# One decoder step on one core: the recurrence and the output projection in another order

## Chip, cores and metric

The kernel runs on one core of one Trainium2 chip. The metric is the device time of one execution in microseconds (us). PE is the matrix engine (PEld its weight loads), DVE the vector engine, ACT the engine for activations, POOL the fourth compute engine, and SP the queue from which all loads and stores are issued. Each engine runs its own program in the order in which it is written, and semaphores hold it until what it needs is there.

## What is computed

One layer of a decoder for 1024 prompt tokens and 8 sample tokens that share all weights. Width 1024, 4 heads of 128, a convolution of 31 taps over 512 channels, 32 experts in 4 groups.

```python
mod = silu(c) @ w_ada + b_ada                     # six rows: shift, scale, gate, twice
h = rms_norm(x, norm1_g) * (1 + sc1) + sh1
z = h @ w_in                                      # q k v o | i f | glu_a glu_b
# heads: per chunk of 128 tokens, state C (128 x 128), n, m for each head
w = exp(dmat - m_t); a_inter = exp(inter - m_t)
s = (q @ k.T) * w
num = s @ v + a_inter * (q @ C); den = sum(s) + a_inter * (q @ n)
hm = num / max(|den|, exp(-m_t))
C = decay * C + (wl * k).T @ v                    # n the same way
hm = layer_norm(hm, mh_norm_g) * sigmoid(o)
# convolution
u = glu_a * sigmoid(glu_b)
hc = silu(layer_norm(causal_conv_31(u) + b_dw))   # norm over the 512 channels
x = x + g1 * (concat(hm, hc) @ w_out)
h2 = rms_norm(x, norm2_g) * (1 + sc2) + sh2
x = x + g2 * hier_moe(h2)                         # best group, best two experts in it
y = rms_norm(x, final_g)
```

The new states, the last 30 convolution inputs and `y` are outputs, for both groups. The prompt starts from zero states; the sample group starts from given ones and takes one token per sequence.

## The kernel before

Tokens stand in 9 tiles: 8 of 128 prompt tokens and one of the 8 samples. The program goes through these stages.

- Conditioning, first norm, and turning `x` (to 54 us). After it `h` lies in SBUF as `hhi` and `hlo`, a coarse and a fine half of each number.
- Projection (54 to 377 us). `project(j)` on PE makes 128 columns of `z` for all 1032 tokens, in 144 matmuls of 344 columns (line 1870): three products of halves. Blocks 0 to 3 are glu_a, 4 to 7 glu_b, then 4 blocks each of q, k, v and o. For each block ACT makes `whi` from the loaded `wraw` (line 1612), DVE makes `wlo` (line 1756), and ACT copies the result out (line 1618). Both halves of the weights have two buffers, so `whi` of block j + 2 follows the end of block j. `z_done`, `whi_ready`, `wlo_ready`, `z_evac` count these steps. Two further groups of conditioning matmuls stand between blocks, and the gate projection behind block 11.
- Beside it on DVE: the 31 taps of the convolution for 4 channel blocks, 4 first taps (line 1781) and 120 of the form "times weight, plus sum" (line 1788), eight per projection block from block 10 on; and `gate_rows` (lines 347 to 374), the running sums and maxima of the gates, behind `wlo` of block 15. Its rows, after three exponentials on ACT, are turned on PE (line 1909) ahead of block 16.
- Reduction of the convolution (377 to 426 us): channel sums on PE with a matrix of ones (lines 719, 739), centring on DVE, squares and a norm on ACT, then a silu. The sigmoids are passes of their own over 4 blocks each.
- Recurrence and output projection (426 to 717 us), a loop over the chunks c. PE makes scores and decay (`inputs`), the part from the state (line 882), numerator (896) and state product (901), then the whole output projection of tile c - 1 (line 822, 32 records), turns the heads of chunk c (911) and `h2` of tile c - 2 (831), and runs the router of tile c - 3 (845). ACT scales the state's part (473, `n2s`), takes the tile's statistics (443 to 445) and copies `h2T` (451). DVE combines the heads, makes `x2 = x + g1 * y` (623, 625) and `h2` (637, 639).
- The sample group's steps hang in that loop as stages: queries against its state `C0` (line 779, 32 single columns), its norms in the small tile `sm`, the outer products (791) in chunks 3 to 6 and, in chunk 7, three broadcasts of modulation rows (762) into the place of `C0`, after the store of the new `C0`. The prompt's three broadcasts stand in chunk 0.
- Routing (730 to 771 us), experts (to 1128 us) and final norm, opened by the mark `stage1_over` on DVE (line 1158) that waits for all stores of this stage.

SP issues the loads in a fixed order too. Behind the projection: the convolution cache `crow`, `wout`, the router's weights and biases, `ntok`, the four parts of `C0`, and then for each tile the load of `x` and the stores of `x2` and `h2`.

Of the kernel before, what the change touches and what calls it, by code (L numbers as in the profile page):

```python
# [67 lines left out]
        "c9T_ps vT_ps gates_ps rowsT_ps mean_ps cT_ps tails_ps cmean_ps sumsq_ps n0T_ps vtok_ps "  # L68
        "qc_ps nnew_ps smean_ps svar_ps rank_ps"),
    "DVE": (  # L70
        "modr_zero dve_consts c9T_ready A1_ready u_ready rows_in csum_ready sB_ready centred conv_sum "
        "centred_s conv_scaled snew_ready sh_ready ssq_ready feats_ready mlstm_done stage1_over "
        "gmax_ready ediff_ready mask_ready glists_ready nov_ready experts_done"),
    "ACT": (
        "csilu softplus_ready srow_ready crstd_ready vtok_ready conv_done nnew_ready srstd_ready "
# [29 lines left out]
def build(nc, x_prompt, x_sample, c_prompt, c_sample, C0, n0, m0, cache, w_ada, b_ada, norm1_g, w_in,  # L105
# [10 lines left out]
    with ExitStack() as ctx:  # L116
# [74 lines left out]
        m0t = sb(st1, "m0t", [H, S])  # L191

# [33 lines left out]
        whi = sb(stB, "whi", [P, 2, KD, P], F32R)  # L226
        stB.close()
# [8 lines left out]
        utail = sb(st1, "utail", [PAD, CB * P])  # L236
        usam = sb(st1, "usam", [S, CB * P])
# [11 lines left out]
        featT = sb(st1, "featT", [P, 2, H, P])  # L249
        featS = sb(st1, "featS", [P, H, S])  # L250
        stL = ExitStack()
        crow = sb(stL, "crow", [4 * PAD, 2, CB * P])
        crstd = sb(stL, "crstd", [P, NTOK])
        cT = sb(stL, "cT", [P, CB, S, CW])
        cprod = sb(stL, "cprod", [P, CB, S, CW])
        stL.close()
        x2 = sb(st1, "x2", [P, 2, D])
        h2 = sb(st1, "h2", [P, D])
        h2T = sb(st1, "h2T", [P, KD, P])
        st1.close()  # L260
# [68 lines left out]
        TAILS, MEAN, YB, BB = 6, 6, 6, (6, 0)  # L329
# [5 lines left out]
        def bcs(i):  # L335

            return z[0:S, U0 + i, 0:D]
# [38 lines left out]
        def act_rest(act, chain):  # L376
# [4 lines left out]
            def conv_squares():  # L381

                act.wait_ge(step("tails_ps"), after("tails_ps"))
                act.activation(utail[:, :], ps[0:PAD, TAILS, :], ACT.Copy).then_inc(sem("tails_ready"), 1)
                act.activation(usam[:, :], ps[0:S, TAILS + 1, :], ACT.Copy).then_inc(sem("tails_ready"), 1)

                act.activation(z[:, U0:U0 + CB, PAD:SC], z[:, GB0:GB0 + CB, PAD:SC], ACT.Square).then_inc(sem("squares"), 1)
                act.wait_ge(step("centred_s"), after("centred_s"))
                act.activation(z[:, U0:U0 + CB, SC:ZW], z[:, GB0:GB0 + CB, SC:ZW], ACT.Square).then_inc(sem("squares"), 1)
                for b in range(H):  # L390
                    act.activation(z[:, O0 + b, PAD:ZW], z[:, O0 + b, PAD:ZW], ACT.Sigmoid).then_inc(sem("sig_o"), 1)
# [63 lines left out]
            for c in range(NC_):  # L455
# [11 lines left out]
                if c == 0:  # L467
                    conv_squares()
# [1484 lines left out]
```

## Time and profile before

| | us |
|---|---|
| runs shown | 1181.47, 1182.86, 1184.37 (median 1182.86) |
| the profiled execution | 1184.33 |
| its span, first to last instruction | 1182.2 |
| PE busy, share of the span | 961.1, 81% |
| DVE busy | 760.3, 64% |
| ACT busy | 502.6, 43% |
| mean granted clock of PE | 0.899 |

The profile gives, for an engine, each instruction's start and duration, and in brackets how long the engine was idle before it and what released it. A record of PE holds a matmul or a part of one. "Granted clock" is the share of full speed that PE was allowed in a stretch: 1.00 is 2.4 GHz, 0.50 is 1.2 GHz.

### The profile page before, as it was taken

The page shows a single profiled execution, that of the slowest core. Times are in us where ns is not written, and L with a number is a line of the kernel's source. Part 1 is how long each engine was busy: PE and PEld are TensorE (multiplying, and loading weights), DVE is VectorE, ACT ScalarE, POOL GpSimd, SP SyncE. Part 2 cuts the span into 40 slices and gives each one's busy share as a digit, 9 for nine tenths or more (in the row PEclk, how much of TensorE's full clock was granted, in tenths as well). Part 3 has the DMA queues.
Part 4 walks back from the last instruction along what each step waited for, and adds up shares of the span by engine and source line. Part 5 has one row for each costly group of instructions (what it writes and reads, how often), then busy time and mean ns, then how long its engine had stood idle before and what let it go on. Part 6 is the DMA issues. An engine that isn't in the chain of part 4 may idle for free. (4 is left out here: it accounts for less than half of the span.)

```text
span 1182.2 us, 12857 instructions
## 1 busy us (share of the span) xinstructions
PE 961.1 (81%) x5013; PEld 770.5 (65%) x5013; DVE 760.3 (64%) x937; ACT 502.6 (43%) x629; POOL 153.1 (13%) x120
## 2 busy tenths in 40 slices
PE   4599999996998779889993890579999999999800
PEld 2398989796997466546562430468888888887700
DVE  3520139499898551625653224879999999998568
ACT  4532231311211540422221010358888888887444
POOL 0100000000000000000000000013443343444300
PEclk9699999997999888979997895689999999999955
DMA  7935311103112420111113007748999999999266
GB/s 284 397 144 206 151 37 36 36 1 72 36 35 64 148 80 1 72 36 55 54 61 117 37 35 157 299 160 352 376 384 384 378 384 380 400 394 358 92 264 255
DMA packets 64758, 213.12 MB, mean 180 GB/s; under 512 B 13840, under 2 KB 34976, under 8 KB 46766
## 3 DMA queue, kind: packets, MB, share of 16 engines
q1 hardware_dynamic: 54334, 195.42, 44.2%
q0 software_dynamic: 10368, 16.93, 3.9%
q8 instruction: 38, 0.62, 0.2%
q14 instruction: 18, 0.15, 0.0%
HBM read 199.14 MB, written 34.49 MB: 198 GB/s over the span
## 5 line engine op out<-in xcount | busy, mean ns | idle before, releaser
L1171 DVE TENSOR_TENSOR elo<-eraw,ehi 128x2048 fp32r<-128x2048 f32 x72 | 161.4, 2283 | 0.0
L1788 DVE SCALAR_TENSOR_TENSOR z<-z,wdT 128x1024 f32<-128x1024 f32 x120 | 144.7, 1279 | 0.1
L1063 ACT ACTIVATE ehi<-eraw 128x2048 fp32r<-128x2048 f32 x72 | 134.0, 1909 | 4.9 <-DMA eraw<-in_w_up 2.5
L1870 PE MATMUL ps<-hhi,whi 128*128 128x344 f32 x576 | 124.8, 326 | 6.4 <-ACT hhi L1640 3.6
L1870 PE MATMUL ps<-hhi,wlo 128*128 128x344 f32 x576 | 124.1, 324 | 0.0
L1870 PE MATMUL ps<-hlo,whi 128*128 128x344 f32 x576 | 122.9, 322 | 0.0
L1618 ACT ACTIVATE z<-ps 128x1032 f32<-128x1032 f32 x24 | 24.8, 1034 | 218.3 <-PE ps L1870 218.3
L1870 PEld LDWEIGHTS ps<-hhi,whi 128*128 128x128 f32 x576 | 98.3, 191 | 8.9 <-issue 8.9
L1756 DVE TENSOR_TENSOR wlo<-wraw,whi 128x1024 fp32r<-128x1024 f32 x22 | 26.9, 1225 | 114.1 <-ACT whi L1612 114.1
L1870 PEld LDWEIGHTS ps<-hhi,wlo 128*128 128x128 f32 x576 | 99.4, 192 | 0.0
L1870 PEld LDWEIGHTS ps<-hlo,whi 128*128 128x128 f32 x576 | 97.3, 190 | 0.0
L1176 DVE TENSOR_TENSOR dlo<-draw,dhi 128x2048 fp32r<-128x2048 f32 x36 | 82.5, 2291 | 0.0
L1380 PE MATMUL ps<-ehi,xhi 128*128 128x512 f32 x288 | 76.7, 409 | 2.1 <-issue 2.1
L1014 POOL DMA_INDIRECT expert_results<-ysb,lists x27 | 72.4, 2681 | 35.4 <-ACT ysb L1089 35.4
L1004 POOL IOTA ioti<- 128x128 int32 x1 | 0.2, 240 | 563.2 <-DVE marks L1158 563.2
L1380 PE MATMUL ps<-ehi,xlo 128*128 128x512 f32 x288 | 72.4, 394 | 0.0
L1380 PE MATMUL ps<-elo,xhi 128*128 128x512 f32 x288 | 71.1, 389 | 0.0
L1069 ACT ACTIVATE dhi<-draw 128x2048 fp32r<-128x2048 f32 x36 | 69.6, 1933 | 0.0
L822 PE MATMUL ps<-wout,featT 128*128 128x512 f32 x128 | 63.1, 650 | 2.8 <-DVE x L625 2.8
L1295 DVE TENSOR_TENSOR xlo<-ps,xhi 128x1024 fp32r<-128x1024 f32 x36 | 44.1, 1225 | 32.0 <-ACT xhi L1073 32.0
L822 PE MATMUL ps<-wout,z 128*128 128x512 f32 (+1 forms) x144 | 63.3, 592 | 0.0
L1380 PEld LDWEIGHTS ps<-ehi,xlo 128*128 128x128 f32 x288 | 54.9, 191 | 12.2
(369 smaller groups left out, 1579.2 us busy)
## 6 DMA issues: line engine op xcount, KB each, us to landing
eraw<-in_w_gate SPq DMA_DIRECT2D x36, 1024.0 KB, 13.5
eraw<-in_w_up SPq DMA_DIRECT2D x36, 1024.0 KB, 16.5
draw<-in_w_down SPq DMA_DIRECT2D x36, 1024.0 KB, 17.1
wada<-in_w_ada SPq DMA_DIRECT2D x24, 1024.0 KB, 10.0
wraw<-in_w_in SPq DMA_DIRECT2D x12, 1024.0 KB, 5.3
y<-expert_results SPq DMA_DIRECT2D x8, 1024.0 KB, 7.9
xt<-in_x_prompt SPq DMA_DIRECT2D x8, 512.0 KB, 5.8
wout<-in_w_out SPq DMA_DIRECT2D x1, 4096.0 KB, 16.0
```

The source lines that it names most:

```text
L822: mm = pe.matmul(ps[0:n, bank + a, :], lhs, wout[:, k, a * 512:(a + 1) * 512], start=(k == 0), stop=(k == KD - 1))
L1014: pool.indirect_dma_start(out=ye_dram, in_=ysb[:, b, :], in_offset=None, out_offset=bass.IndirectOffsetOnAxis(ap=at, axis=0), bounds_check ...
L1063: act.activation(ehi[:, s % 2, i, :, :], eraw[:, s, i, :, :], ACT.Copy).then_inc(sem("ehi_ready"), 1)
L1069: act.activation(dhi[:, s % 2, :, :], draw[:, s, :, :], ACT.Copy).then_inc(sem("dhi_ready"), 1)
L1171: dve.tensor_tensor(elo[:, s, i, :, :], eraw[:, s, i, :, :], ehi[:, s % 2, i, :, :].bitcast(F32), ALU.subtract)\
L1176: dve.tensor_tensor(dlo[:, s, :, :], draw[:, s, :, :], dhi[:, s % 2, :, :].bitcast(F32), ALU.subtract)\
L1295: dve.tensor_tensor(xlo[:, b, :, :], ps[:, 0:2, :].rearrange("p a (k n) -> p (a k) n", k=4), xhi[:, b, :, :].bitcast(F32), ALU.subtract).t ...
L1380: mm = pe.matmul(ps[:, 2, :].rearrange("p (i f) -> p i f", i=2), x[:, b, k, :], w[:, :, k, :], start=(i + k == 0), stop=(i == 2 and k == K ...
L1618: act.activation(z[:, j, PAD:ZW].rearrange("p (c n) -> p c n", c=3), ps[:, 3 * v:3 * v + 3, 0:TW], ACT.Copy).then_inc(sem("z_evac"), 1)
L1756: dve.tensor_tensor(wlo[:, u, :, v * P:(v + 1) * P], wraw[:, u, :, v * P:(v + 1) * P], whi[:, v, :, :].bitcast(F32), ALU.subtract).then_in ...
L1788: dve.scalar_tensor_tensor(out=z[:, GB0 + b, PAD:SC], in0=z[:, U0 + b, w:w + T], scalar=wdT[:, b, w:w + 1], in1=z[:, GB0 + b, PAD:SC], op0 ...
L1870: mm = pe.matmul(ps[0:n, bank + c, 0:TW], w(k), h[:, k, c * TW:(c + 1) * TW], start=first, stop=last)
```

## The change

**Convolution.** ACT writes sigmoids straight out of the accumulators for blocks 4 to 7 and 20 to 23. DVE forms the gate product of each channel block when that block is out, and taps begin with the first block. `gate_rows` moves one block earlier. The blocks 16 to 23 are written one by one, with the sample group's convolution, tails and the channel means between them.

**Loop.** The output projection of a tile is cut into the half over the convolution's channels (`out_conv`) and the half over the heads (`out_heads`), with the turning of the heads and the router between. ACT takes the tile statistics ahead of the state's scaling, and waits with them for the store and the turning of the `h2` before (before, `tile_x2` on DVE waited for these). The products in `x2` stay in the accumulators. The outer products move to chunks 1 to 4.

**Rest.** Each broadcast of a modulation row is 8 turns instead of 8 matmuls; the sample group's three go to another place in `z` and are spread over the tail. The cache loads stand earlier on SP.

```diff
-            return z[0:S, U0 + i, 0:D]
+            return z[0:S, K0 + i, 0:D]
...
             def tile_stats(i, n):
                 act.wait_ge(sem("x2_ready"), i + 1)
+                if i:
+                    act.wait_ge(sem("h2_out"), 16 * i)
+                    act.wait_ge(sem("h2T_ps"), i)
...
+            for c in range(1, NC_):
+                decay(c)
+                values(c)
+                if c >= 2:
+                    head_rstd(c - 1)
...
+                if c <= 4:
+                    c0_scale(c)
+                tile_stats(c - 1, P)
+                from_state(c)
                 if c >= 2:
                     tile_h2T(c - 2, P)
-            for i in range(NC_ - 2, NT):
-                tile_stats(i, rows[i])
-                tile_h2T(i, rows[i])
+            broadcast(1, 0, bcs(0))
...
+            for c in range(1, NC_):
                 if c >= 2:
+                    state(c - 1)
+                if 2 <= c <= 5:
+                    c0_update(c - 1)
+                if c >= 2:
+                    heads(c - 1)
+                scores(c)
+                if c >= 2:
+                    head_scale(c - 1)
+                    feats(c - 1)
+                if c == 1:
+                    sample_centre()
+                if c == 2:
+                    sample_feats()
+                if c >= 3:
+                    tile_logits(c - 3, P)
+                if c >= 2:
+                    tile_h2(c - 2, P)
+                tile_x2(c - 1, P)
...
+            def broadcast(k, i):
+
+                src, at = ((modT, 2 * KD), (A2, 0), (modT, 3 * KD))[i]
+                for q in range(KD):
+                    if k == 0:
+                        rows_in_ = src[:, at + q, 0:1].broadcast_to([P, P])
+                        mm = pe.transpose(ps[:, BB[0] + q // 4, (q % 4) * P:(q % 4 + 1) * P], rows_in_, ident[:, :])
                     else:
+                        mm = pe.transpose(ps[0:S, BB[1] + q // 4, (q % 4) * P:(q % 4 + 1) * P], src[:, at + q, 1:9], ident[:, :])
+                mm.then_inc(sem("bcv_ps"), 1)
...
+            pe.wait_ge(sem("z_evac"), NZ + 1)
+            inputs(0)
+            conv_squares()
+            from_state(0)
+            state(0)
+            pe.wait_ge(step("crstd_ready"), after("crstd_ready"))
+            numerator(0)
+            broadcast(0, 0)
+            pe.wait_ge(sem("n2_ready"), 4)
+            pe.wait_ge(sem("n0_in"), 16)
+            pe.transpose(ps[:, 0, 0:S * H], ntok[:, :], ident[0:S * H, 0:S * H]).then_inc(step("n0T_ps"), 1)
...
+            for c in range(1, NC_):
+                pe.wait_ge(sem("n2_ready"), 4 * c)
+                if c == 1:
+                    pe.wait_ge(step("vtok_ready"), after("vtok_ready"))
...
+                inputs(c)
+                out_conv(c - 1)
                 if c >= 2:
-                    pe.wait_ge(sem("caug_ready"), 1 + H * (c + 1))
+                    heads_turned(c - 1)
...
+                if c >= 3:
+                    router(c - 3, P)
+                out_heads(c - 1)
+                from_state(c)
+                state(c)
...
+                numerator(c)
+                if c <= 4:
+                    pe.wait_ge(sem("x2_ready"), c)
+                    for b in (2 * c - 2, 2 * c - 1):
+                        pe.matmul(ps[:, YB + b % 2, :], on_all(b, S), vtok[:, :], start=True, stop=True)\
+                          .then_inc(sem("vB_ps"), 1)
+                if c >= 2:
                     h2_transpose(c - 2, P)
+            pe.wait_ge(sem("n2_ready"), 4 * NC_)
+            broadcast(1, 0)
+            out_conv(NC_ - 1)
+            pe.wait_ge(sem("bcv_ready"), 4)
+            broadcast(1, 1)
+            heads_turned(NC_ - 1)
             router(NC_ - 3, P)
-            out_proj(NC_ - 1, P)
+            out_heads(NC_ - 1)
+            pe.wait_ge(sem("bcv_ready"), 5)
+            broadcast(1, 2)
...
+            load(crow[:, :, :], cache.rearrange("(g b) w c -> (b w) g c", g=2), "crow_in")
+            load(conv_s[:, 0:PAD - 1, :], cache[:, 1:PAD, :], "out_done")
...
+            sp.wait_ge(sem("tails_ready"), 1)
+            load(conv_p, utail[0:PAD, :], "tails_out")
+            load(conv_s[:, PAD - 1, :], utail[PAD:PAD + S, :], "tails_out")
             sp.wait_ge(sem("z_done"), NZ + 2)
...
+                               ACT.Sigmoid if GB0 <= j < Q0 or j >= O0 else ACT.Copy).then_inc(sem("z_evac"), 1)
...
+            blocks(16, 20)
+            act.wait_ge(step("tails_ps"), after("tails_ps"))
+            act.activation(utail, ps[0:PAD + S, 7, :], ACT.Copy).then_inc(sem("tails_ready"), 1)
+            blocks(20, 21)
+            act.wait_ge(sem("tails_out"), 32)
+            blocks(21, 22)
+            act.wait_ge(step("conv_sum"), after("conv_sum"))
+            evac(22)
+            act.wait_ge(step("centred_s"), after("centred_s"))
+            act.activation(csq[:, :, :], z[:, GB0:GB0 + CB, SC:ZW], ACT.Square).then_inc(sem("squares"), 1)
+            for k in range(2):
+                act.wait_ge(sem("centred"), k + 1)
+                act.activation(z[:, U0:U0 + CB, 512 * k:512 * (k + 1)], z[:, GB0:GB0 + CB, PAD + 512 * k:PAD + 512 * (k + 1)],
+                               ACT.Square).then_inc(sem("squares"), 1)
+            evac(23)
...
+            def glu(b):
+                dve.wait_ge(sem("z_evac"), 2 + GB0 + b + 1)
+                chain(dve.tensor_tensor(z[:, U0 + b, PAD:ZW], z[:, U0 + b, PAD:ZW], z[:, GB0 + b, PAD:ZW], ALU.mult))
...
+            glu(0)
+            taps(5, 1)
             lo(7)
+            glu(1)
+            taps(7, 2)
             lo(8)
+            glu(2)
+            taps(7, 3)
             lo(9)
-
...
+            glu(3)
+            taps(28, 4)
             for j in range(10, NZ):
                 lo(j)
                 if j == 13:
                     modulation(2)
                     norm_factor(A2, 4 * KD, MB + KD)
-                if j == 15:
+                    taps(6, 4)
+                if j == 14:
                     gate_rows(dve, chain)
-                taps(2 * (j - 10) + 1)
-                taps(2 * (j - 10) + 2)
-            for w in range(2 * (NZ - 10) + 1, CW):
-                taps(w)
-
-            dve.wait_ge(sem("conv_taps"), CB * CW)
+                elif j == 18:
+                    rows_turned(dve, chain)
+                    taps(7, 4)
+                elif j == 19:
+                    sample_conv(dve, chain)
+                    taps(4, 4)
+                elif j < 22:
+                    taps(8, 4)
+                if j == 22:
+                    dve.wait_ge(step("cmean_ps"), after("cmean_ps"))
+                    chain(centre(dve, SC, ZW, ps[:, 6, 0:S]))
+                    dve.memset(mark(), 0.0).then_inc(step("centred_s"), 1)
+                if j >= 22:
+                    out_gate(dve, chain, j - 22)
+            taps(CB * CW, 4)
...
+            project(16, 0, 0)
+            project(17, 0, 1)
+            sample_conv_turns(pe)
+            project(18, 1, 0)
+            project(19, 1, 1)
+            conv_tails(pe)
+            project(20, 0, 0)
+            project(21, 0, 1)
+            project(22, 1, 0)
+            conv_mean(pe)
```

DVE beside projection blocks 7 to 12: `wlo` is the fine half of a block's weights, SCALAR_TENSOR_TENSOR a tap. Before:

```order
L1756 TENSOR_TENSOR wlo<-wraw,whi 128x8x128 x3
L1775 MEMSET z 128x4x30
L1777 TENSOR_TENSOR z<-z 128x4x1032
L1778 MEMSET marks 1x1
L1781 TENSOR_SCALAR z<-z,wdT,vT 128x1024 x4
L1756 TENSOR_TENSOR wlo<-wraw,whi 128x8x128
L1788 SCALAR_TENSOR_TENSOR z<-z,wdT 128x1024 x8
L1756 TENSOR_TENSOR wlo<-wraw,whi 128x8x128
```

After:

```order
L1817 TENSOR_TENSOR wlo<-wraw,whi 128x8x128
L1830 TENSOR_TENSOR z<-z 128x1032
L1840 TENSOR_SCALAR z<-z,wdT,vT 128x1024
L1844 SCALAR_TENSOR_TENSOR z<-z,wdT 128x1024 x6
L1817 TENSOR_TENSOR wlo<-wraw,whi 128x8x128
L1830 TENSOR_TENSOR z<-z 128x1032
L1840 TENSOR_SCALAR z<-z,wdT,vT 128x1024
L1844 SCALAR_TENSOR_TENSOR z<-z,wdT 128x1024 x27
L1817 TENSOR_TENSOR wlo<-wraw,whi 128x8x128
```

The first row before is `wlo` of blocks 7 to 9, the second `wlo` there is block 10's. The rows after begin with `wlo` of block 8; the gate product of the last channel block and 28 taps now stand between those of blocks 9 and 10, where one product over four blocks and four first taps stood.

ACT in one chunk of the loop: `wx` is the decay, `vaug` the values, `n2s` the scaled part from the state, `h` with `ssq` the tile's statistics, `lst` the heads' norm. Before:

```order
L460 ACTIVATE wx<-ps,rowsT 128x128 x4
L465 ACTIVATE vaug<-ps 128x4x128
L473 ACTIVATE n2s<-ps,rowsT 128x130 x4
L443 ACTIVATE h,ssq<-x 128x1024
L444 ACTIVATE ssq<-ssq,epst 128x1
L445 ACTIVATE ssq<-ssq 128x1
L482 ACTIVATE lst<-bag,epst 128x4
L483 ACTIVATE lst<-lst 128x4
L451 ACTIVATE h2T<-ps 128x1024
```

After:

```order
L428 ACTIVATE wx<-ps,rowsT 128x128 x4
L435 ACTIVATE vaug<-ps 128x4x128
L448 ACTIVATE lst<-bag,epst 128x4
L449 ACTIVATE lst<-lst 128x4
L411 ACTIVATE h,ssq<-x 128x1024
L412 ACTIVATE ssq<-ssq,epst 128x1
L413 ACTIVATE ssq<-ssq 128x1
L443 ACTIVATE n2s<-ps,rowsT 128x130 x4
L419 ACTIVATE h2T<-ps 128x1024
```

`n2s` moved behind the statistics, and the heads' norm, now of the chunk before, ahead of them.

PE in the last chunk and the first part of the tail: `modT` and `A` are modulation rows (the broadcasts), `wout` marks the projection, `hn` the heads, `h` the second norm's result. Before:

```order
L901 MATMUL ps<-vaug,kw 128x130 x4
L762 MATMUL ps<-ident,modT 8x128 x8
L762 MATMUL ps<-ident,A 8x128 x8
L762 MATMUL ps<-ident,modT 8x128 x8
L822 MATMUL ps<-wout,featT 128x512 x8
L822 MATMUL ps<-wout,z 128x512 x8
L911 MATMUL ps<-ident,hn 128x128 x4
L831 MATMUL ps<-ident,h 128x128 x8
L845 MATMUL ps<-wr,h2T 128x36 x8
```

After:

```order
L833 MATMUL ps<-vaug,sT 128x130 x4
L872 MATMUL ps<-ident,h 128x128 x8
L788 MATMUL ps<-ident,modT 8x128 x8
L848 MATMUL ps<-wout,z 128x512 x8
L788 MATMUL ps<-ident,A 8x128 x8
L840 MATMUL ps<-ident,hn 128x128 x4
L884 MATMUL ps<-wr,h2T 128x36 x8
L848 MATMUL ps<-wout,z 128x512 x8
L788 MATMUL ps<-ident,modT 8x128 x8
```

The three broadcasts stood one behind the other ahead of a whole projection; now they stand around its two halves, which are the two `wout` rows.

## Rows read from the trace of the kernel before

**Rows 1.** Busy time by stretch: stretch, length, each engine's busy time, clock, DMA share, GB/s.

```profile
426.00:612.00 186.00, 165.50 (x701) 105.95 (x702) 88.01 (x212) 47.49 (x131) 0.00 (x0) 0.89 0.12 43
612.00:730.00 118.00, 72.07 (x311) 38.61 (x309) 33.33 (x46) 17.23 (x35) 0.00 (x0) 0.80 0.25 57
```

**Rows 2.** What PE waited for, 377 to 731: total, times, longest, in us.

```profile
PE ps L762 <- ACT z L414: 19.6, 2, 18.5
PE ps L791 <- ACT sm L435: 9.4, 1, 9.4
...
PE ps L896 <- DVE logits L644: 7.5, 5, 1.5
```

**Rows 3.** Timeline, DVE and ACT beside blocks 7 to 10: start, us, instruction, [idle before].

```profile
157.09 1.23 DVE L1756 TENSOR_TENSOR wlo<-wraw,whi 128x1024 fp32r<-128x1024 f32 x1 [10.13 <-ACT whi L1612]
...
175.65 1.23 DVE L1756 TENSOR_TENSOR wlo<-wraw,whi 128x1024 fp32r<-128x1024 f32 x1 [5.82 <-ACT whi L1612]
176.79 9.65 DVE L1788 SCALAR_TENSOR_TENSOR z<-z,wdT 128x1024 f32<-128x1024 f32 x8
...
185.00 1.03 ACT L1618 ACTIVATE z<-ps 128x1032 f32<-128x1032 f32 x1 [9.38 <-PE ps L1870]
```

**Rows 4.** Timeline: end of the gate rows (DVE), next weights (ACT), rows' turn (PE).

```profile
264.19 0.06 DVE L374 MEMSET marks<- 1x1 f32 x1
...
274.46 1.06 ACT L1612 ACTIVATE whi<-wraw 128x1024 fp32r<-128x1024 f32 x1 [15.29 <-DMA wraw<-in_w_in]
...
279.92 1.17 PE L1909 MATMUL ps<-ident,rows 68*128 68x68 f32 x8 [10.47 <-ACT marks L1680]
```

**Rows 5.** Timeline: end of the projection (ACT) and chunk 0's numerator (PE).

```profile
377.08 1.03 ACT L1618 ACTIVATE z<-ps 128x1032 f32<-128x1032 f32 x1 [10.32 <-PE ps L1870]
...
411.98 1.13 PE L896 MATMUL ps<-vaug,sT 128*128 128x130 f32 x8 [2.55 <-ACT crstd L399]
```

**Rows 6.** Timeline: `ntok` on SP, and the sample queries on PE.

```profile
394.67 1.23 SPq L1447 DMA_DIRECT2D ntok<-in_state_mlstm_n  x1
...
438.48 11.42 PE L779 MATMUL ps<-z 128*128 128x1 f32 x64
```

**Rows 7.** DMA issues, 370 to 480: times, KB each, us from issue to landing.

```profile
z<-in_state_mlstm_C SPq DMA_DIRECT2D x4, 512.0 KB, 6.1
```

**Rows 8.** Timeline, PE and ACT in chunks 5 to 7 of the loop.

```profile
566.82 1.98 PE L791 MATMUL ps<-vtok,ident 8*128 8x512 f32 x4
...
583.88 1.06 PE L857 MATMUL ps<-z 128*128 128x128 f32 x8
...
612.00 1.06 PE L857 MATMUL ps<-z 128*128 128x128 f32 x8
...
621.52 1.91 PE L762 MATMUL ps<-ident,modT 128*8 128x128 f32 x16
...
618.10 1.15 ACT L473 ACTIVATE n2s<-ps,rowsT 128x130 f32<-128x130 f32 x4 [2.08 <-PE ps L882]
619.34 1.06 ACT L443 ACTIVATE h<-x 128x1024 f32<-128x1024 f32 x1
...
620.85 0.20 ACT L445 ACTIVATE ssq<-ssq 128x1 f32<-128x1 f32 x1
```

**Rows 9.** Timeline, PE: the numerators of two chunks, each behind a wait.

```profile
536.67 2.07 PE L896 MATMUL ps<-vaug,sT 128*128 128x130 f32 x8 [1.50 <-DVE logits L644]
...
564.86 1.13 PE L896 MATMUL ps<-vaug,sT 128*128 128x130 f32 x8 [1.50 <-DVE logits L644]
```

**Rows 10.** Busy time by stretch, columns as in rows 1, for the granted clock.

```profile
428.00:430.00 2.00, 1.48 (x13) 1.12 (x11) 0.00 (x0) 2.00 (x2) 0.00 (x0) 1.00 0.04 8
...
538.00:540.00 2.00, 2.00 (x11) 2.00 (x11) 0.70 (x1) 0.17 (x1) 0.00 (x0) 0.50 0.26 107
```

**Rows 11.** Timeline, DVE: the last `h2`, and the mark that opens routing.

```profile
715.55 1.87 DVE L639 TENSOR_TENSOR h<-h,z 8x1024 f32<-8x1024 f32 x1
...
730.18 0.06 DVE L1158 MEMSET marks<- 1x1 f32 x1 [10.02 <-DMA out<-caug]
```

More of the change, by code:

```diff
@@ L191, in build @@
         m0t = sb(st1, "m0t", [H, S])
+        csq = sb(st1, "csq", [P, CB, S])
         stA = ExitStack()
@@ new lines, in sample_conv @@
+        def sample_conv(dve, chain):
+            zs = z[:, GB0:GB0 + CB, SC:ZW]
+            dve.wait_ge(step("cT_ps"), after("cT_ps"))
+            for g in range(2):
+                chain.last(dve.tensor_copy(
+                    cT[:, :, 4 * g:4 * g + 4, 0:PAD],
+                    ps[:, 6 + g, 0:4 * 4 * PAD].rearrange("p (k b w) -> p k b w", k=CB, b=4)))
+            chain(dve.tensor_copy(cT[:, :, :, PAD], z[:, U0:U0 + CB, SC:ZW]))
+            dve.memset(mark(), 0.0).then_inc(step("cT_copied"), 1)
+            for b in range(CB):
+                chain.last(dve.tensor_tensor(cprod[:, b, :, :], cT[:, b, :, :],
+                                             wdT[:, b:b + 1, :].broadcast_to([P, S, CW]), ALU.mult))
+            chain.wait()
+            chain(dve.tensor_reduce(zs, cprod[:, :, :, :], AXX, ALU.add))
+            chain(dve.tensor_tensor(zs, zs, vT[:, VB:VB + CB].rearrange("p (b o) -> p b o", o=1).broadcast_to([P, CB, S]), ALU.add))
+            dve.memset(mark(), 0.0).then_inc(step("conv_sum"), 1)
@@ L516, in dve_rest, with out_gate, signal @@
+        def out_gate(dve, chain, h):
+            dve.wait_ge(sem("z_evac"), 2 + O0 + h + 1)
+            chain.last(dve.tensor_scalar(z[:, O0 + h, PAD:ZW], z[:, O0 + h, PAD:ZW], vT[:, VM + h:VM + h + 1], None, ALU.mult))
+        def dve_rest(dve, chain):
+            def signal(name):
+                chain.wait()
+                dve.memset(mark(), 0.0).then_inc(step(name) if name in STEP else sem(name), 1)
+            zc = z[:, GB0:GB0 + CB, :]
             dve.wait_ge(step("mean_ps"), after("mean_ps"))
@@ new lines, in channel_sums, with conv_tails @@
+        def channel_sums(pe, out, rhs):
+            for b in range(CB):
+                mm = pe.matmul(out, ones[:, :], rhs(b), start=(b == 0), stop=(b == CB - 1))
+            return mm
+        def conv_tails(pe):
+            pe.wait_ge(step("cT_copied"), after("cT_copied"))
+            for b in range(CB):
+                mm = pe.transpose(ps[0:PAD + S, 7, b * P:(b + 1) * P], z[:, U0 + b, T:ZW], ident[:, :])
+            mm.then_inc(step("tails_ps"), 1)
+            pe.wait_ge(step("conv_sum"), after("conv_sum"))
+            channel_sums(pe, ps[:, 6, 0:S], lambda b: z[:, GB0 + b, SC:ZW]).then_inc(step("cmean_ps"), 1)
@@ new lines, in pe_rest @@
+            state(0)
+            pe.wait_ge(step("crstd_ready"), after("crstd_ready"))
[4 more added lines that the diff above has]
+            pe.transpose(ps[:, 0, 0:S * H], ntok[:, :], ident[0:S * H, 0:S * H]).then_inc(step("n0T_ps"), 1)
+            for h in range(H):
+                mm = pe.transpose(ps[0:S, 1, h * DH:(h + 1) * DH], z[:, V0 + h, SC:ZW], ident[:, :])
+            mm.then_inc(step("vtok_ps"), 1)
```

639 lines of the change are left out of this document (282 added, 357 removed).

## The prediction

> **What bounds the kernel now.** I read the busy time by stretch first. Up to 377 us the matrix engine runs the 24 projection blocks almost without a pause, and after 730 us nothing is edited, so that part only shifts. Between lie two stretches in which it is not full [rows 1]: chunks 1 to 6 have 165.50 us of work in 186, at a mean granted clock of 0.89, and the last chunk with the tail has 72.07 in 118, at 0.80. The list of waits names the largest holes [rows 2]: 19.6 us for the sample group's broadcasts (18.5 of it in one wait), 9.4 us for the sample group's small tile `sm`, and five waits of 1.5 us, one in each of five chunks. The reader is to see that PE sets the pace where it is full, and that elsewhere the order on ACT and DVE sets it. The profiled execution took 1184.33 us with a span of 1182.2, so 2.1 us lie around the span; it is 1.5 us over the median of 1182.86. I work out a difference of spans and take it from the median.
>
> **Part 1, the taps.** Before, the order on DVE is `wlo` of block 9 at 157.09, then the gate products, then `wlo` of block 10 at 175.65, then eight taps in 9.65 us, 1.21 each [rows 3]. PE needs block 10's `wlo` when block 9 ends, at 185.0, where ACT copies block 9 out [rows 3]: 185.0 - 175.65 - 1.23, so 8.1 us of slack. After, 28 taps stand between these two `wlo` (the first is a cheaper scalar multiply). Seven of them belong to one channel block and follow each other on the same data, which I put at the 1.21 of a row plus a little. From 158.3: one gate product of 1.15, 28 taps of 1.21 or 34 to 35, and `wlo` 1.15, so it is ready at about 194.5. **PE stands for 9.5 us where it had no wait, and I add 1.5 for the slower clock behind the hole (priced below): +11.** Behind PE queue the remaining 14 blocks. The later groups of eight taps (9.65) fit into a block of 11.4 us, so the stall does not repeat.
>
> **Part 2, gate rows one block earlier.** They now stand behind `wlo` of block 14 instead of 15. Before, they ended at 264.19; only then may SP store the maxima and fetch the next weights, which ACT got at 274.46, and PE waited 10.47 us for the exponentials [rows 4]. With the +11 the rows end again near 264, the weights land again near 274, but block 15 ends at 280 instead of 269.4, so weights are no longer last. What is last is ACT's evacuation, one copy and three exponentials behind block 15, 4.7 us. PE waits 4.7 instead of 10.47: -5.8. Without the stall the same step would give -6.1, so the stall and this gain do not cancel.
>
> Into the projection come pieces that stood behind it: 12 turns, eight 8-column sums and two 512-column sums. At the rates of the rows in [rows 8, 9] (a record of 130 columns 0.14, one of 512 about 0.44) they come to about 4 us. The projection ended at 377.08 [rows 5]; now 377.1 + 11 - 5.8 + 4, about 386.5. The sigmoids move into evacuations that ACT does anyway with over 9 us idle before each [rows 3]: nothing, even with an extra table load. The early loads of the cache go to SP before the second set of conditioning weights, where PE had no wait: nothing, at worst their own issue of about a microsecond.
>
> **Part 3, from projection to chunk 2.** Before, the numerator of chunk 0, which waits for the channel norm, began at 411.98 [rows 5], 34.9 us behind the projection. After, means, centring and squares are done while block 23 runs. PE then has the inputs of chunk 0 (3.2) and the sums of squares (24 records, 16 of them as wide as a projection half, 7.9), so sums end at 397.6 and the norm is there 2.4 later, at 400. That is 12 us earlier, and most of it is lost again. The sample group's C0 loads are issued on SP behind the output weights, the router's loads and `ntok`. Before, `ntok` was issued 17.6 us behind the projection's end, at 394.67 [rows 6]. After, two loads are gone from ahead of it: 16.3, so it is issued by 403, four C0 loads follow by 407, and land 6.1 later [rows 7], at 412.5 to 413. PE stands at the sample queries until then, and these took 11.42 us of mostly slow single-column work [rows 6] that the change does not shrink: 424. Chunk 1 starts at 426.4, within half a microsecond of before. Its inputs 3.2, two halves 7.0 each, three small groups of 1.0, the outer products 1.98 and ACT's statistics give chunk 2's start at about 450.7.
>
> **Part 4, one chunk.** PE's work before, from 612.00 to 621.52 less one wait of 1.5, is 8.0 for inputs, router and three small groups; from 566.82 to 583.88 it is 17.1 with the outer products of 2.0 in it [rows 8]. That makes 23.1 without and 25.1 with them. After, they stand in chunks 1 to 4. What is new is a wait at each chunk's end: ACT now does the tile statistics ahead of the scaling of the state's part, and waits with them for the turned `h2` of the tile before. So when PE has turned `h2`, ACT needs 619.34 to 621.05, 1.7 us, for statistics and 1.15 for scaling [rows 8]; with hops, 3.1 us of PE's idle time. Ahead of the turn PE waits some 1.0 for `x2` (2.4 on DVE) and the state's update (1.1), where no outer products cover it. A chunk takes 27.1, or 28.1 with outer products. Behind ACT's waiting statistics are queued exactly this scaling and the copy of `h2T`, and behind them PE's next chunk. Chunks 2, 3, 4 at 28.0 and 5, 6 at 27.1 end at 450.7 + 138.2, about 588, against 612.00 [rows 8]. The halves around the heads cover the heads' path on DVE (about 10 us of PE work over 8), and the 9.4 wait is gone since no sample step is late.
>
> **The clock.** After the 1.50 wait at 536.67 eight records took 2.07, after the same wait at 564.86 they took 1.13 [rows 9]; the granted clock in 538 to 540 is 0.50, the lower level of 1.2 GHz [rows 10]. Such a fall cost about 1.6 (this group and the next). New waits of 3 us are longer than that, so I take a fall after each: seven at 1.2 us, +8 by the end of the tail. Bounds: 0 and 7 x 1.6 = 11.
>
> At one place a page speaks against the change. The six broadcasts become turns of eight records instead of matmuls of 16, which took 1.91 [rows 8]: about 0.95 each. In 428 to 430 PE did mostly turns and the granted clock was 1.00 [rows 10], so I count them at the full clock. The Trainium skill, "TensorE: Matmul & The Clock Gate", section "Part 4: PE-mode transpose", says that the full clock does not engage for transposes. The trace disagrees in that stretch; what the rule would give is rival (f).
>
> **Part 5, the tail.** The broadcasts' target no longer is the C states' store, so the 18.5 wait goes [rows 2]. From chunk 7's start, forward: inputs to numerator, the halves of tile 6 and the turn 24.1; scaling 3.1; broadcast, half, heads, router, half, broadcast, turn and router 22.5; the sample tile's 14.0; then `x2` 2.6, statistics 1.8, tile 7's `h2T` copy and router 2.8, and 3.9 for the last `h2`: 74.8. On this last piece PE is the late one only through the router. The last `h2` before ended at 717.42, and the mark that opens routing stood 12.8 later, at 730.18, on the state's store [rows 11]. That store is still the last in SP's queue: 588 + 74.8 + 12.8 = 675.5, and with the clock's 8 some 683.5. The product written in place into the accumulators instead of to SBUF costs between nothing and another 1.2 per tile; I take nothing, since the product before read the same accumulators.
>
> **Sum.** 730.18 - 683.5 = 46.7, less rounding 46: 1182.86 - 46, **1137 us**.
>
> **Rivals.** (a) *No stall*: if DVE does the 28 taps in the slack, or if some wait ahead of block 10 hides it, 11 come back: 1126. Against it: between `wlo` of block 9 and the end of block 9 DVE has 26.7 us, and the gate product, 28 taps and `wlo` need 36. (b) *The clock holds* through 3-us waits, as it did after the second of the two waits in [rows 9]: 1129; with (a) 1118. (c) *The chunk is longer than summed*: a hop more on the chain x2, turn, statistics, scaling, or C0 landing later, or a fall that lasts. Two us in each of seven chunks is 14: 1151. (d) *Slower than before*: statistics now wait for the store of the `h2` before. By my order that `h2` is written about 16.7 us after a chunk's start and statistics want it 6 us later. If a store took over 12.6 us, each further us costs seven. Six us of cover and 46/7 = 6.6 more is the point of no gain; at 15 us for a store the kernel would be at 1182.86 - 46 + 7 x 9 = 1200. Against it: 512 KB of C0 land in 6.1 [rows 7] on queues that are quieter in the chunks. (e) *It does not do what it says*: halves turn late because the heads' path on DVE, with eight state updates ahead of it, outlasts inputs and half; then each chunk keeps its old length of 26.6 to 28.1 plus the new waits, and only the tail gains, most of which the stall and the clock take: near 1180. (f) *Turns at the lower clock level*: six broadcasts at 1.9 instead of 0.95, +5.5, so 1142. Against it is the granted clock of 1.00 in a stretch of turns [rows 10].
>
> **How the numbers follow.** Forecast 0.53, (a) 0.09, (b) 0.13, (c) 0.17, (d) 0.03, (e) 0.02, (f) 0.03. The range has to hold the forecast with its own bounds (clock 0 to 11, in-place products 0 to 9), (a), (b) and most of (c): 1118 to 1156. A measurement of this kernel tells 0.3% from no change, 3.5 us. Faster: all but (d) and (e), 0.95; same 0.02, slower 0.03.
>
> **What would show it.** One PE wait of 9 to 10 us on DVE's `wlo` near 185; projection's end near 386.5; PE waiting on DMA for C0 near 410; one 3-us PE wait per chunk, released by ACT's scaling, with half clock behind it; no wait of 9 or 18 us; routing's mark near 683. I am wrong on part 1 if block 10 starts without a wait, on part 4 if chunk starts are not 27 to 30 us apart, and on part 5 if the tail from chunk 7's start to the mark is not 88 to 95.

## The result, and the profile after

The changed kernel takes 1146.07 us (median of four runs, 1145.27 to 1146.96) against 1183.61 for the kernel before (median of four). The ratio is 0.9679, with a 95% interval of 0.9661 to 0.9697. The forecast was 1137, so the direction and the range held, and the gain was 37.5 us instead of 46. The profiled execution took 1145.27, its span 1143.3; the mean granted clock was 0.903.

Set beside the prediction, place by place (us from the start of the span):

| place | before | predicted | after |
|---|---|---|---|
| PE's wait ahead of block 10 | none | 9.5 | 9.60 |
| PE's wait ahead of the rows' turn | 10.47 | 4.7 | 4.56 |
| projection ends | 377.1 | 386.5 | 385.4 |
| sample queries begin, and take | 438.5, 11.42 | 412.5 to 413, 11.42 | 409.4, 13.81 |
| chunk 1 begins | 426.0 | 426.4 | 426.0 |
| chunk 2 begins | 466.5 | 450.7 | 449.0 |
| chunk 7 begins | 612.0 | 588, and 6 for the clock | 600.2 |
| routing opens | 730.2 | 683.5 | 693.75 |

Up to chunk 2 each place is met within 2 us, apart from the queries. From chunk 2 on the kernel is slower than forecast: by 10 us at the mark that opens routing.

The table also shows where the gain lies. Chunk 2 begins 17.5 us earlier than before, and the tail from chunk 7's start to the mark is 24.7 us shorter. Between the two, from chunk 2 to chunk 7, the kernel before took 145.5 us and the changed one takes 151.2: the loop itself became slower.

What PE waited for from 54 to 720 (total, times, longest):

```profile
PE ps L793 <- ACT n2s L443: 15.4, 6, 2.9
PE ps L1955 <- issue: 9.6, 1, 9.6
PE ps L892 <- DMA z<-in_state_mlstm_C: 5.8, 1, 5.8
PE ps L884 <- ACT h2T L419: 5.6, 3, 4.2
PE ps L1994 <- ACT marks L1726: 4.6, 1, 4.6
PE ps L872 <- DVE h L632: 4.1, 1, 4.1
```

Against [rows 2], the waits of 18.5 and 9.4 us and the five of 1.5 are gone. In their place stand the forecast ones: six waits ahead of a chunk for ACT's scaling (line 793 is the first matmul of a chunk; the first of them is 0.77 us, five are 2.92, and one more of 2.92 stands ahead of the tail's first broadcast), the stall ahead of block 10 (line 1955), and the loads of C0.

The stall on PE's timeline (start, us, instruction, idle before). PE has no releaser to show for it, but DVE makes `wlo` of block 10 from 192.54 to 193.75, and PE goes on at 193.86. The first experiment below takes the stall away:

```profile
183.64 0.62 PE L1955 MATMUL ps<-hlo,whi 128*128 128x344 f32 x3
193.86 1.20 PE L1955 MATMUL ps<-hhi,whi 128*128 128x344 f32 x3 [9.60 <-issue]
194.86 1.06 PE L1955 MATMUL ps<-hhi,wlo 128*128 128x344 f32 x3
...
198.15 0.63 PE L1955 MATMUL ps<-hlo,whi 128*128 128x344 f32 x3
```

Three records take 1.06 behind the stall, and 0.63 from 198.15 on: that is the lower clock level, worth 1.9 us in this block.

One chunk, from PE's timeline. It begins at 477.85, and the next at 508.99:

```profile
477.85 0.61 PE L793 MATMUL ps<-causal,identb 128*128 128x512 bf16 x1 [2.92 <-ACT n2s L443]
478.39 2.07 PE L796 MATMUL ps<-negM,ident 4*128 4x128 f32 x8
480.39 2.08 PE L800 MATMUL ps<-z 128*128 128x128 f32 x8
482.26 1.06 PE L809 MATMUL ps<-ident,z 128*128 128x128 f32 x4
483.12 1.06 PE L812 MATMUL ps<-ident,z 128*128 128x128 f32 x4
483.97 7.39 PE L848 MATMUL ps<-wout,z 128*128 128x512 f32 x16
...
504.98 1.09 PE L872 MATMUL ps<-ident,h 128*128 128x128 f32 x8
508.99 0.61 PE L793 MATMUL ps<-causal,identb 128*128 128x512 bf16 x1 [2.92 <-ACT n2s L443]
```

The wait of 2.92 is the predicted 3.1. But the inputs of the chunk, from 477.85 to 483.97, take 6.1 us, where the prediction had 3.2 plus 1.2 for the clock. ACT's timeline shows who holds the chunk back: statistics first (lines 411 to 413), begun when PE has turned `h2`, then the scaling (443).

```profile
506.19 1.06 ACT L411 ACTIVATE h<-x 128x1024 f32<-128x1024 f32 x1 [19.47 <-PE ps L872]
...
507.70 0.20 ACT L413 ACTIVATE ssq<-ssq 128x1 f32<-128x1 f32 x1
507.81 1.13 ACT L443 ACTIVATE n2s<-ps,rowsT 128x130 f32<-128x130 f32 x4
508.81 1.04 ACT L419 ACTIVATE h2T<-ps 128x1024 f32<-128x1024 f32 x1
```

Here the reader sees 19.47 us of idle time on ACT, and then 2.9 us of work for which PE stands. Busy time by stretch (columns as in [rows 1]) shows the clock at the start of the chunk at 477.85:

```profile
478.00:480.00 2.00, 2.00 (x8) 1.61 (x8) 1.83 (x6) 0.71 (x1) 0.00 (x0) 0.50 0.00 0
480.00:482.00 2.00, 2.00 (x10) 1.78 (x9) 1.91 (x10) 1.14 (x4) 0.00 (x0) 0.50 0.00 0
482.00:484.00 2.00, 2.00 (x12) 2.00 (x11) 0.69 (x1) 0.64 (x2) 0.00 (x0) 0.50 0.00 0
484.00:486.00 2.00, 2.00 (x5) 0.88 (x5) 1.29 (x2) 1.97 (x8) 0.00 (x0) 0.83 0.00 0
```

For 6 us PE is full and runs at 1.2 GHz, the lower level. In the places behind a 1.5 us wait from which I took the price, [rows 9, 10], the fall was over in less than 4.

The tail, to be set beside [rows 11]:

```profile
681.40 1.88 DVE L632 TENSOR_TENSOR h<-h,z 8x1024 f32<-8x1024 f32 x1
...
693.75 0.06 DVE L1207 MEMSET marks<- 1x1 f32 x1 [7.73 <-DMA out<-caug]
```

From chunk 7's start to the mark are 93.5 us; before they were 118.2.

### The profile page after: what moved, and what is told of

It reads as the page before. It is cut to its first block and busy times, and to the rows that moved or that the text cites. A ratio compares the mean times of both kernels' runs of the same rounds, so it can differ in the third digit from the quotient of the medians.

```text
span 1143.3 us, 12727 instructions
## 1 busy us (share of the span) xinstructions
PE 958.4 (84%) x4961; PEld 775.7 (68%) x4961; DVE 763.2 (67%) x939; ACT 492.4 (43%) x621; POOL 156.3 (14%) x120
## 5 line engine op out<-in xcount | busy, mean ns | idle before, releaser
L848 PE MATMUL ps<-wout,z 128*128 128x512 f32 (+1 forms) x288 | 132.3, 614 | 0.5 <-DVE z L690 0.5
L1667 ACT ACTIVATE z<-ps 128x1032 f32<-128x1032 f32 x24 | 24.8, 1033 | 228.9 <-PE ps L1955 228.9
L848 PEld LDWEIGHTS ps<-wout,z 128*128 128x128 f32 (+1 forms) x288 | 52.4, 188 | 68.1 <-issue 67.4
L1063 POOL DMA_INDIRECT expert_results<-ysb,lists x27 | 72.5, 2685 | 35.2 <-ACT ysb L1138 35.2
L411 ACT ACTIVATE h<-x 128x1024 f32<-128x1024 f32 (+1 forms) x9 | 9.5, 1054 | 144.7 <-PE ps L872 112.2
```

The costliest lines, as they stand in the source:

```text
L848: mm = pe.matmul(ps[0:n, bank + a, :], lhs, wout[:, k, a * 512:(a + 1) * 512], start=(k == H), stop=(k == H - 1))
L1063: pool.indirect_dma_start(out=ye_dram, in_=ysb[:, b, :], in_offset=None, out_offset=bass.IndirectOffsetOnAxis(ap=at, axis=0), bounds_check ...
```

## Experiments

All edits are to the changed kernel, one each but for the last. Times are medians of four runs (five for the work in the waits), the interval is that of the ratio to the kernel before, and the changed kernel stands at 1146.07 and 0.9661 to 0.9697. It did not run again beside them. The kernel before did, with medians of 1182.52 beside the first four and 1184.54 beside the last four, so two or three us between medians decide nothing without the trace.

**Fewer taps ahead of block 10.**

```diff
-            taps(28, 4)
+            taps(19, 4)
```

> The changed kernel with 19 instead of 28 taps between the fine halves of blocks 9 and 10; the nine others fall to DVE's groups beside blocks 20 and 21. Theory (the taps make the stall): the 9.6 us wait ahead of block 10 goes to under 0.5, block 10 loses its first 4 us at half clock (1.9 us), the wait ahead of the rows' turn stays near 4.6 because ACT's evacuation of block 15 is last there; the projection ends 11 us earlier, at about 374.5, and the time is 1146 - 11 = 1135. Rival (the nine taps are late elsewhere): the channel means then wait for DVE behind block 22, and the time is 1140 to 1146.

Measured: 1137.66 us, 0.9592 (0.9547 to 0.9637). The stall is gone from the list of waits, the rows' turn still waits 4.6, and the projection ends at 373.72 instead of 385.41, so the theory's 11 us are there (11.7). The medians differ by 8.4, the profiled spans by 8.5 and the ratios by 10.3. In the trace 2.6 us are given back in chunk 1, not where the rival put them:

```profile
414.24 0.63 PE L793 MATMUL ps<-causal,identb 128*128 128x512 bf16 x1
414.80 2.07 PE L796 MATMUL ps<-negM,ident 4*128 4x128 f32 x8
416.80 2.08 PE L800 MATMUL ps<-z 128*128 128x128 f32 x8
418.67 1.06 PE L809 MATMUL ps<-ident,z 128*128 128x128 f32 x4
```

The four groups at the lower level take 2.07 and so on; in the changed kernel, from 426.53 on, PE had come back to the full clock there, and the same group of line 796 took 1.20. Same work, no wait, 2.6 us more. That need not be the taps' doing: the profiled execution of the work in the waits below has all 28 taps and the same slow groups in chunk 1 (2.07 and 2.08 from 429.75 on). Why the clock comes back there in one execution and not in another is not shown.

**ACT's scaling ahead of the statistics.**

```diff
-                tile_stats(c - 1, P)
                 from_state(c)
                 if c >= 2:
                     tile_h2T(c - 2, P)
+                tile_stats(c - 1, P)
```

> The changed kernel with ACT's scaling of the state's part and the copy of the turned h2 put ahead of the tile statistics, as before the change. Theory (each chunk's wait costs itself and a clock fall behind it): the six waits of 2.92 before a chunk go, the granted clock behind them stays at 1.00, and the inputs of a chunk take 3.2 instead of 6.1; a wait of about 1 comes in its place for the copy of the turned h2. Chunks 25 to 27 us apart instead of 30.3, time 1146 - 6 x 5 = 1116 (1112 to 1122). Rival A (only the wait counts, the clock falls anyway, as it does behind the 0.77 wait ahead of chunk 2): chunks 28, time 1131. Rival B (h2 gets later, and router and statistics wait in its place): chunks unchanged at 30, time 1143 to 1148.

Measured: 1110.05 us, 0.937 (0.9326 to 0.9414), 2 us under the theory's range. The six waits of 2.92 are gone altogether, and the one that I had expected in their place did not come. One chunk of PE's timeline:

```profile
498.30 1.09 PE L872 MATMUL ps<-ident,h 128*128 128x128 f32 x8
499.23 0.38 PE L793 MATMUL ps<-causal,identb 128*128 128x512 bf16 x1
499.54 1.15 PE L796 MATMUL ps<-negM,ident 4*128 4x128 f32 x8
500.62 1.16 PE L800 MATMUL ps<-z 128*128 128x128 f32 x8
501.62 0.60 PE L809 MATMUL ps<-ident,z 128*128 128x128 f32 x4
502.06 0.60 PE L812 MATMUL ps<-ident,z 128*128 128x128 f32 x4
502.49 7.03 PE L848 MATMUL ps<-wout,z 128*128 128x512 f32 x16
```

and its busy time by stretch, for chunks 2 to 6:

```profile
448.00:574.00 126.00, 123.42 (x547) 76.94 (x545) 79.44 (x179) 34.04 (x105) 0.00 (x0) 0.97 0.18 66
```

The inputs take 3.26 us, 499.23 to 502.49. Two falls of the clock are left: in chunk 2 (the last section shows it), and in chunk 6 behind the 1.03 us for the state's update. Chunks 3 to 7 begin 24.8 us apart on the mean (474.39 to 573.72, four chunks), where they were 30.6 apart (477.85 to 600.21). So this one line of order, which the change had turned round, cost about 36 us of what the rest of the change could bring. The tail is shorter too: 83.6 instead of 93.5 from chunk 7's start to the mark, since its inputs and its first halves run at the full clock and the wait of 2.92 ahead of its first broadcast is gone.

**Work in the waits.** Nobody reads the result of these matmuls.

```diff
                     h2_transpose(c - 2, P)
+                    pe.wait_ge(sem("x2_ready"), c)
+                    pe.wait_ge(sem("cnew_ready"), 2 * H * min(c, 4))
+                    for _ in range(10):
+                        pe.matmul(ps[:, YB, 0:P], ident[:, :], ident[:, :], start=True, stop=True)
```

> The changed kernel with ten extra matmuls of 128 columns, whose result nobody reads, on PE in each of the six waits of 2.92 at a chunk's end. The waits' length stays, but PE works in them (2.2 of 2.9 us). Theory (idle time makes the clock fall, and the fall costs 3 us per chunk, twice what I had counted): granted clock 1.00 at each chunk's start, inputs in 3.2 instead of 6.1, chunks 27 to 28 apart, time 1146 - 18 = 1128 (1124 to 1132). Rival (the slow inputs are not from the idle time but from what ACT and DVE do beside them, or the clock falls all the same): no change, 1144 to 1149.

Measured: 1129.93 us, 0.9537 (0.9491 to 0.9582): 16 us less than the changed kernel, though each chunk has 2.4 us more of work in it. Four of the five runs lie between 1129 and 1133. The profiled one took 1137.99: its projection ends 3 us later than the changed kernel's, and more of its chunks 1 and 2 runs at the lower level, so I read it from chunk 3 on:

```profile
512.28 2.47 PE L957 MATMUL ps<-ident 128*128 128x128 f32 x20 [0.53 <-DVE z L602]
514.67 0.39 PE L793 MATMUL ps<-causal,identb 128*128 128x512 bf16 x1
514.99 1.15 PE L796 MATMUL ps<-negM,ident 4*128 4x128 f32 x8
...
569.70 0.39 PE L793 MATMUL ps<-causal,identb 128*128 128x512 bf16 x1 [0.69 <-ACT n2s L443]
...
571.10 1.59 PE L800 MATMUL ps<-z 128*128 128x128 f32 x8
572.48 1.06 PE L809 MATMUL ps<-ident,z 128*128 128x128 f32 x4
```

Chunks 3 to 7 are 27.9 us apart (486.75 to 598.46), 2.7 less than without this filler. That is the price of the clock alone, and the rest of the 5.8 that the order costs per chunk, 3.1, is the wait. The medians say the same without a choice of chunks: 16.1 us over six waits, 2.7 each. Even so the clock fell once more from chunk 3 on, in the chunk at 569.70, behind a wait of 0.69.

**C0 ahead of the router's weights.**

```diff
+            sp.wait_ge(step("sumsq_ps"), after("sumsq_ps"))
+            for i in range(4):
+                load(z[:, U0 + i, 0:8 * DH].rearrange("p (x e) -> p x e", x=8),
+                     C0[2 * i:2 * i + 2].rearrange("b h d e -> d (b h) e"), "c0_in")
             load(wr[:, :, 0:NG], w_grp.rearrange("(p k) n -> p k n", p=P), "wr_in")
...
             load(rbias[:, NG:NR], b_er.rearrange("(o n) -> o n", o=1).broadcast_to([P, NE]), "wr_in")
-            sp.wait_ge(step("sumsq_ps"), after("sumsq_ps"))
-            for i in range(4):
...
```

`ntok` thereby stands right behind `wout`.

> The changed kernel with the sample group's state loads on SP ahead of the router's weights and biases (whose two slow issues take 11 us), behind the sums of squares that free their place. Theory (the 5.8 us wait for them is on the path): they are issued from 396.6 on and land by 406, PE waits 0 to 3 for them instead of 5.8, and the queries' 13.8 us fall to 11 to 13; time 1146 - 5 = 1141 (1138 to 1143). Rival (the first projection half or the tile loads wait in their place, since x of the first tiles is then issued 10 us later): 1145 to 1148.

Measured: 1143.49 us, 0.9643 (0.9598 to 0.9688), which overlaps the changed kernel's interval, so the times alone decide nothing. In the trace the wait for C0 is 3.3 us instead of 5.8, and chunk 2 begins at 446.60 instead of 449.01. So the wait was on the path, but half of it stayed: the loads, issued from 397.30 on (expected: 396.6), let PE go on at 407.27. The queries did not fall to 11 to 13 us either, they took 13.81 as before this edit. The time is a miss by 2 us.

**Gate rows behind block 15 again.**

```diff
-                if j == 14:
+                if j == 15:
                     gate_rows(dve, chain)
```

> The changed kernel with the gate rows back behind block 15's fine half instead of block 14's. Theory (the prediction's -5.8 for that step): the rows end 11.4 us later, the next weights land behind block 15's end, and PE waits about 11 us ahead of the rows' turn instead of 4.6: time 1146 + 6 = 1152 (1150 to 1154). Rival (the step did nothing, since the order of taps around it sets the rows' end): 1145 to 1148.

Measured: 1154.44 us, 0.9728 (0.9697 to 0.9759). The wait ahead of the rows' turn is 9.70 instead of 4.56, and ACT's `whi` waits for the weights again, as in [rows 4]:

```profile
287.53 1.06 ACT L1661 ACTIVATE whi<-wraw 128x1024 fp32r<-128x1024 f32 x1 [14.52 <-DMA wraw<-in_w_in]
...
293.00 1.17 PE L1994 MATMUL ps<-ident,rows 68*128 68x68 f32 x8 [9.70 <-ACT marks L1726]
```

So the step saves 5.1 us of waiting, against 5.8 forecast. The medians differ by 8.4, half a us past the theory's range, the ratios by 5.8. The evacuations of blocks 11 and 12 are 28.9 us apart in this execution and 26.2 in the changed kernel's, with the same wait of 2.9 between them: 2.7 are a clock fall behind the gates that the changed kernel did not have in its execution.

**Broadcast rows back in C0's place.**

```diff
-            return z[0:S, K0 + i, 0:D]
+            return z[0:S, U0 + i, 0:D]
...
+            act.wait_ge(sem("c_out"), 64)
             broadcast(1, 0, bcs(0))
```

> The changed kernel with the sample group's broadcast rows back in the place of C0, so that ACT waits for the store of the new states again. Prediction's step (the other place removed the 18.5 us wait): the wait comes back in part, 3 to 10 us ahead of ACT's first copy, time 1149 to 1156. Rival (the later place of the broadcasts in PE's and ACT's order removed it: the store is issued at 620 and lands near 631, and ACT wants the rows at 631.7): 1145 to 1148.

Measured: 1150.32 us, 0.9714 (0.967 to 0.9759), with runs from 1147.78 to 1156.91. The median lies in the range of the prediction's step, but the interval of the ratio overlaps the changed kernel's, so the times don't separate the two. The trace does: ACT waits for PE and not for the store,

```profile
633.31 1.01 ACT L396 ACTIVATE z<-ps 8x1024 f32<-8x1024 f32 x1 [0.28 <-PE ps L789]
```

and from chunk 7 (601.81) to the mark (695.03) it takes 93.2 us, as in the changed kernel (93.5). The rival holds: the later order alone keeps the 18.5 us of [rows 2] away, and the new place is not needed for it. SP issues the states' store 20 us behind chunk 7's start (at 622.03), and PE makes the rows 30 us behind it (at 632.16); before, it was 18 us for the store (630.33) and 9.5 for the rows (621.52). The new place in the old order was not run.

**The projection in one piece.**

```diff
                 inputs(c)
-                out_conv(c - 1)
                 if c >= 2:
                     heads_turned(c - 1)
...
                     router(c - 3, P)
+                out_conv(c - 1)
                 out_heads(c - 1)
```

> The changed kernel with both halves of a tile's projection behind the turning of the heads and the router, in one piece. Theory (the first half covers the heads' path on DVE): PE waits for the heads in each chunk; in the changed kernel they are ready 1.5 us behind the end of the inputs, so at least 6 x 1.6 = 10 more, and with a second clock fall of up to 3 us each, 1156 to 1174. Rival (the slow inputs already cover the heads): 1145 to 1149.

Measured: 1170.87 us, 0.9867 (0.9834 to 0.99). PE's list of waits has a new row,

```profile
PE ps L840 <- DVE hn L684: 8.4, 6, 1.5
```

so 8.4 us of waits cost 24.8 of time. Chunks 3 to 7 are 35.2 us apart (479.03 to 619.76): 4.6 more each, of which 1.4 is the wait. The rest is the clock, as the projection behind it shows (both halves of a tile take 15.3 to 16.9 in chunks 3 to 6, 16.88 in the one shown, where they take 13.98 at the full clock in chunk 1):

```profile
486.55 0.66 PE L840 MATMUL ps<-ident,hn 128*128 128x128 f32 x4 [1.38 <-DVE hn L684]
...
489.22 16.88 PE L848 MATMUL ps<-wout,z 128*128 128x512 f32 x32
```

Cutting the projection in halves is therefore worth 25 us here (22 by the ratios).

**Together**: 19 taps, scaling first, C0 first, and on DVE the sample tile's `h2` ahead of the seventh tile's logits.

```diff
             tile_x2(NC_, S)
-            tile_logits(NC_ - 1, P)
             tile_h2(NC_, S)
+            tile_logits(NC_ - 1, P)
             tile_logits(NC_, S)
```

> The changed kernel with four edits: 19 taps ahead of block 10, ACT's scaling ahead of the statistics, C0 loads ahead of the router's weights, and the sample tile's h2 ahead of the seventh tile's logits on DVE (4.1 us wait for the last h2). Theory (the gains stand in different stretches and add): 1110 - 8.4 - 2.6 - 4.6 = 1094 (1089 to 1099). Rival (a clock fall at another place gives part of it back, as it did with the 19 taps alone): 1100 to 1106.

Measured: 1093.83 us, 0.9231 (0.9198 to 0.9263), 52.2 us below the changed kernel. The three edits that also ran alone gained 8.4, 36.0 and 2.6 there, 47.0 in sum; 5.2 are left over. The fourth was not run alone, but the tail shows it: from chunk 7's start (560.51) to the mark are 79.1 us, where the scaling first alone left 83.6, and the wait of 4.1 ahead of the last `h2`'s turn is gone from the list. So 4.4 of the 5.2 are the fourth edit. Chunk 1 begins at the full clock here, so the loss that stood there with the 19 taps does not come back. The mark stands at 639.62, 54 us earlier than in the changed kernel. This version beats both.

## Why the prediction was right, and where it was off

**Part 1, the taps: right.** 9.60 us of stall and 1.9 behind it, against 9.5 and 1.5. Nineteen taps end it, and the projection then ends 11.7 us earlier, so the cause is shown.

**Part 2, gate rows: right.** The wait fell to 4.56, and undoing the step brings 5.1 us of it back. The projection's end, worked out as a sum of four terms, was met within 1.1 us.

**Part 3, up to chunk 2: right in sum, by luck: two errors nearly cancel.** C0 landed 3 us earlier than summed, because SP's two slow issues took 8.09 and 3.10 us, where they took 9.81 and 4.34 before. The queries took 13.81, not the 11.42 of [rows 6]. That row was not at one level: its first records ran at the full clock. With the new wait ahead of them, of 3.2 to 5.8 us, they took 13.8 in every version, so "the change does not shrink it" should have read "and behind a wait it takes longer"; no version runs them without the wait.

**Part 4, the chunk: the mechanism right, the term for the clock too small.** The new wait was named with its cause, engine and length (3.1 against 2.92), and the waits for the state's update came as well. What failed is "The clock": 1.2 us for a fall, with 1.6 as the upper bound. The filler shows 2.7 per chunk, the timeline 2.9 in the inputs alone. I had taken the price from a fall behind a wait of 1.5 and said myself that the new waits were longer, but let that speak only for whether the clock falls, not for how long. Five chunks from 449.01 to 600.21 took 151.2; the sum with its 1.2 gave 144. These 7 us are most of the miss. The six falls behind waits of 2.92, at 2.7 each, make 16, past the bound of 11 for the clock; the time stayed in the range because the range also had room for rival (c). By the prediction's own sign this part is wrong: chunk starts were to be 27 to 30 us apart, and they are 28.8, 31.1, 30.9, 30.0 and 30.3. A slip beside it is small: 450.7 and 138.2 make 588.9, not 588.

**Part 5, the tail: the length right within 4 us, one reason not borne out.** 93.5 us against 87.6 and some 2 for the clock. The inputs of chunk 7 took 2.5 more than at the full clock, the half behind the broadcast 8.73 instead of 7.0, the sample tile 15.60 instead of 14. The prediction put the end of the 18.5 us wait down to the broadcasts' other place. With the old place the wait does not come back, so their later place in the order is enough for it.

**The range and the rivals.** The time lies in the range and between the forecast and rival (c), which named 1151 for a longer chunk or "a fall that lasts". Rival (a) was wrong, (b) too: the clock fell behind each wait of 2.92. Rival (d), the store of `h2`, shows in no list of waits. Rival (e) named a chunk of the old length plus the new waits, and about that came (30.6), but not by its cause: no wait for the heads stands in the list. Rival (f): the broadcasts took 1.04 for eight turns, 0.87 from start to start, at the full clock (1.00 from 640 to 641) and 1.91 where it was low (0.50 from 423 to 425). The Trainium skill, "TensorE: Matmul & The Clock Gate", section "Part 4: PE-mode transpose", says that the full clock does not engage for transposes. The trace disagrees for turns that stand between matmuls; a stream of nothing but turns was not run.

What stays open: why the clock falls behind some short waits and not behind others, and at times behind none. It fell behind 0.77 ahead of chunk 2 in the changed kernel and held behind three of the 1.5 us waits before; the executions differ in it from run to run.

## What to carry to other kernels

When an edit puts a wait on a full matrix engine, price it as the wait plus what the same work costs at half clock behind it, and take that second part from the shape and length of the work that stands there, not from a shorter wait elsewhere; here a 2.9 us wait cost 5.8. Before changing the order of a side engine that has 19 us of idle time per round, ask which of its results the pacing engine needs next, and put that one first. A wait whose releaser is a store may be a matter of order in the queue rather than of memory: look at when the store was issued.

## What the runs showed of the hardware that was not expected

A matrix engine without any idle time can run at the lower level. In the changed kernel the 64 single-column records of the queries fill every stretch, and the granted clock stays down in all six stretches of 2 us from 411 to 423; two of them:

```profile
411.00:413.00 2.00, 2.00 (x11) 2.00 (x11) 0.67 (x1) 0.85 (x1) 0.00 (x0) 0.50 0.01 4
...
421.00:423.00 2.00, 2.00 (x11) 2.00 (x11) 0.00 (x0) 0.00 (x0) 0.00 (x0) 0.50 0.00 0
```

In the kernel before, the clock even fell from 1.00 to 0.50 in the middle of these records, with PE busy throughout:

```profile
438.00:440.00 2.00, 2.00 (x21) 2.00 (x20) 1.57 (x8) 0.00 (x0) 0.00 (x0) 1.00 0.00 0
...
442.00:444.00 2.00, 2.00 (x11) 2.00 (x11) 1.54 (x6) 0.50 (x2) 0.00 (x0) 0.50 0.00 0
```

It falls without a wait in wide matmuls too. With ACT's scaling first, PE has no idle time from 409.90 to 461, and the granted clock is 1.00 from 427 to 450; then, in chunk 2, it falls to 0.50 (452 to 454). The group of line 809 takes 1.06, where it takes 0.60 at the full clock:

```profile
450.01 1.39 PE L800 MATMUL ps<-z 128*128 128x128 f32 x8
451.19 1.06 PE L809 MATMUL ps<-ident,z 128*128 128x128 f32 x4
```

So idle time is one thing behind which the clock falls, as the work in the waits shows, but not the only one. And the waits of 1.4 us for the heads (the projection in one piece) cost three times their length: ahead of the one shown the clock was at 1.00 again (485 to 486.5) and it fell behind it, and in the next chunk it stayed at 0.50 from 520 to 528.
